# Deeper softmax lookahead in the attention and another order around the first mLSTM chunk, in a two-layer hybrid encoder step

## The reference

```python
def _attend(q, k, v, bias, sinks):
    s = jnp.einsum('...qkgd,...skd->...kgqs', q.astype(jnp.float32), k.astype(jnp.float32))
    s = s * (B_HEAD_DIM ** -0.5) + bias
    sink = jnp.broadcast_to(sinks.astype(jnp.float32)[:, :, None, None], s.shape[:-1] + (1,))
    p = jax.nn.softmax(jnp.concatenate([s, sink], axis=-1), axis=-1)[..., :-1]
    return jnp.einsum('...kgqs,...skd->...qkgd', p, v.astype(jnp.float32))
...
    num = jnp.einsum('nhts,nshd->nthd', s, v) + w_prev.transpose(0, 2, 1)[..., None] * jnp.einsum('nthd,nhde->nthe', q, c_m)
    den = s.sum(axis=-1) + w_prev * jnp.einsum('nthd,nhd->nht', q, n_m)
    norm = jnp.maximum(jnp.abs(den), jnp.exp(-m_t))
    h = num / norm.transpose(0, 2, 1)[..., None]
...
    c_new = decay[..., None, None] * c_m + jnp.einsum('nhs,nshd,nshe->nhde', ws, k, v)
```

## Time and profile before

| | us |
|---|---|
| median of 3 runs (lowest, highest) | 2728.79 (2726.03, 2731.42) |
| the profiled execution | 2728.37 |
| its span, from first to last instruction | 2726.6 |
| PE busy in it | 2655.8 |

### The profile page before, as it was taken

The page is one execution under the profiler, slowest core; times in us unless marked ns, Lnnn a source line. Parts: engine busy times, 40 slices in busy tenths (PEclk is TensorE's granted clock), DMA queues, the critical chain, the costliest instruction groups (busy, mean ns, idle before and its releaser), DMA issues.

```text
span 2726.6 us, 40949 instructions
## 1 busy us (share of the span) xinstructions
PE 2655.8 (97%) x17188; PEld 2591.4 (95%) x17188; DVE 1452.7 (53%) x2384; ACT 605.0 (22%) x1276; POOL 942.2 (35%) x439
## 2 busy tenths in 40 slices
PE   8997999999999999999999989999999999999997
PEld 7896799999999999999999967899999999999997
DVE  7976654444444444657764048654444444444566
ACT  4544331000000000133122147431000000000043
POOL 3321223333333333333433310124333333333430
PEclk9998999999999999999999999999999999999999
DMA  4101211111111111113132232411111111111111
GB/s 144 50 24 56 72 39 47 47 47 47 47 47 47 47 47 47 47 47 127 41 92 93 93 103 84 141 32 55 47 41 45 47 47 47 47 47 47 54 40 64
DMA packets 65487, 162.48 MB, mean 60 GB/s; under 512 B 7696, under 2 KB 36368, under 8 KB 64408
## 3 DMA queue, kind: packets, MB, share of 16 engines
q1 hardware_dynamic: 34224, 114.12, 13.3%
q10 hardware_dynamic: 31080, 45.75, 5.0%
HBM read 139.43 MB, written 20.42 MB: 59 GB/s over the span
## 4 chain that ended last, share of the span: by engine, by line
PE 89%; DVE 5%; ACT 2%; issue 2%; DMA 0%; ACTq 0%; POOL 0%; DVEq 0%; POOLq 0%
PE ps L449 29%; PE ps L451 28%; PE ps L450 28%; PE ps L965 1%; DVE uc L1285 1%; PE ps L690 1%; PE ps L672 1%; DVE ss L1372 1%; DMA ob<-vod 0%; PE ps L895 0%; DVE lr L1308 0%; PE ps L930 0%; PE ps L551 0%; ACT dw L2075 0%; PE ps L656 0%
## 5 line engine op out<-in xcount | busy, mean ns | idle before, releaser
L449 PE MATMUL ps<-xh,wh 128*128 128x352 f32 x3432 | 1119.3, 326 | 21.5 <-DVE xl L1001 12.6
L450 PE MATMUL ps<-xl,wh 128*128 128x352 f32 x3432 | 1112.4, 324 | 0.0
L451 PE MATMUL ps<-xh,wl 128*128 128x352 f32 x3432 | 1112.3, 324 | 0.0
L528 POOL TENSOR_TENSOR wh<-raw,seeds 128x1024 fp32r<-128x1024 f32 x199 | 407.2, 2046 | 1460.2 <-PE ps L451 1424.6
L449 PEld LDWEIGHTS ps<-xh,wh 128*128 128x128 f32 x3432 | 649.9, 189 | 29.7 <-issue 24.3
L450 PEld LDWEIGHTS ps<-xl,wh 128*128 128x128 f32 x3432 | 650.0, 189 | 1.7
L451 PEld LDWEIGHTS ps<-xh,wl 128*128 128x128 f32 x3432 | 649.7, 189 | 0.0
L530 POOL TENSOR_TENSOR wl<-raw,wh 128x1024 fp32r<-128x1024 f32 x208 | 525.3, 2526 | 133.6 <-ACT wh L1693 110.0
L1116 DVE TENSOR_TENSOR tmpa<-ps,rstd 128x352 f32<-128x352 f32 x132 | 69.1, 524 | 719.7 <-PE ps L451 710.8
L449 PE MATMUL ps<-hh,wh 128*128 128x352 f32 x1056 | 340.4, 322 | 0.0
L451 PE MATMUL ps<-hh,wl 128*128 128x352 f32 x1056 | 340.0, 322 | 0.0
(11 more groups left out here) (265 smaller groups left out, 2340.6 us busy)
## 6 DMA issues: line engine op xcount, KB each, us to landing
raw<-wstream SPq DMA_DIRECT2D x208, 512.0 KB, 3.6
vod<-stage ACTq DMA_DIRECT2D x72, 128.0 KB, 1.9
vb<-vod ACTq DMA_DIRECT2D x9, 512.0 KB, 4.1
ob<-vod ACTq DMA_DIRECT2D x9, 512.0 KB, 4.4
x<-xT ACTq DMA_DIRECT2D x2, 2112.0 KB, 8.3
xsave<-x ACTq DMA_DIRECT2D x1, 4224.0 KB, 13.1
x<-xsave ACTq DMA_DIRECT2D x1, 4224.0 KB, 12.6
yT<-ybuf SPq DMA_DIRECT2D x6, 704.0 KB, 3.3
```

The lines of the kernel that those rows point to most:

```text
L449: pe.matmul(out, whi, mhi, start=first, stop=False)
L450: pe.matmul(out, whi, mlo, start=False, stop=False)
L451: return pe.matmul(out, wlo, mhi, start=False, stop=last)
L528: pool.tensor_tensor(hi, raw[:, r, :], zero, ALU.add).then_inc(hi_made, 1)
```

## The change

1. **Attention.** `scores` run two blocks ahead of the transposes rather than one; ss gets four buffers (`ss[h % 4]`) and `biased(h)` waits for the transposes of h - 4. The order on DVE and ACT follows; fill 7 moves from behind block 1 to the A place of block 2, fill 14 and 13 one place forward. `maxima` takes two instructions in place of three, with the sinks negated once beforehand (`nsink`). POOL's splits in the attention stay POOL's.
2. **First mLSTM chunk.** `load_v(0)` and `load_decays(0)` are issued before the O half of the V/O phase; `load_o(0)` goes behind `powers(0)`. POOL's `mask(1)` comes right behind `mask(0)`, ahead of the splits of two weight blocks. The four `c_o` DMAs go from ACT's queue to SP's.
3. **End of the mLSTM.** The last chunk's transposes stand behind unit 2 of the output projection, not behind unit 1.

```diff
-        FILL_A = {0: 4, 1: 6, 4: 9, 5: 11, 6: 12, 7: 13}
-        FILL_B = {0: 5, 1: 7, 3: 8, 4: 10, 7: 14, 8: 15}
+        FILL_A = {0: 4, 1: 6, 2: 7, 4: 9, 5: 11, 6: 12, 7: 14}
+        FILL_B = {0: 5, 3: 8, 4: 10, 6: 13, 8: 15}
...
+                    if NRAW * i + j == B1_OUT + NW:
+                        sp.wait_ge(cup_read, 1 + 8)
+                        for half in range(2):
+                            for f in range(2):
+                                sp.dma_start(half_tile(O["c_o"][1], half, f), state_half(cs, half, f)).then_inc(c_sent, 16)
...
                 if b == B1_OUT + 2:
                     mask(0)
+                    mask(1)
...
-                    if last_chunk is not None and u == 2:
+                    if last_chunk is not None and u == 3:
                         pe.wait_ge(cl_ready, 1 + 2 * (CH - 1))
                         transpose_h(last_chunk)
...
                     transpose_p(2 * n)
-                    if n + 1 < NQ:
-                        scores(n + 1)
+                    if n + 2 < NQ:
+                        scores(n + 2)
                     transpose_p(2 * n + 1)
...
-                step(dve.scalar_tensor_tensor(r[0], r[0], 0.125, sink, ALU.mult, ALU.max))
-                step(dve.tensor_scalar(r[1], r[0], -1.0, None, ALU.mult))
-                dve.tensor_tensor(r[2], sink, r[0], ALU.subtract).then_inc(nm_ready, 1)
+                step(dve.scalar_tensor_tensor(r[1], r[0], -0.125, nsink[0:w, 4 * kvh:4 * kvh + 4], ALU.mult, ALU.min))
+                dve.tensor_tensor(r[2], sink, r[1], ALU.add).then_inc(nm_ready, 1)
...
             for n in range(NQ):
-                a, b = 2 * n + 2, 2 * n + 3
                 if n + 1 < NQ:
-                    biased(a)
-                    maxima(a)
-                    biased(b)
+                    shares(2 * n + 2)
+                if n + 2 < NQ:
+                    biased(2 * n + 4)
+                    maxima(2 * n + 4)
+                if n + 1 < NQ:
+                    shares(2 * n + 3)
                 filled(FILL_A.get(n))
-                if n + 1 < NQ:
-                    maxima(b)
-                    shares(a)
+                if n + 2 < NQ:
+                    biased(2 * n + 5)
+                    maxima(2 * n + 5)
...
             for n in range(NQ):
                 copy_p(2 * n)
                 copy_p(2 * n + 1)
+                if n == 0:
+                    exps(2)
+                    exps(3)
...
-                if n + 1 < NQ:
-                    exps(2 * n + 2)
+                if n + 2 < NQ:
+                    exps(2 * n + 4)
...
             for half, func in ((0, ACT.Copy), (1, ACT.Sigmoid)):
+                if half == 1:
+
+                    for j in range(2):
+                        act.wait_ge(stage_out[j], 16 + 16 * CH * 2)
+                    load_v(0)
+                    act.wait_ge(arow_sent, 16)
+                    load_decays(0)
...
             act.wait_ge(acc_free, FREE0["vo1"] + 72)
             keys_queries(0)
             powers(0)
+            for j in range(2):
+                act.wait_ge(stage_out[j], 16 + 16 * CH * 4)
+            load_o(0)
             chunk(0, None, 1)
```

More of the change, by code:

```diff
@@ L166, in build @@
         lr4 = at("lr4", o_x + 4 * TOK + 2 * CA, [P, CA])
-        ss = at("ss", m, [P, 2, 4, 2 * P])
+        ss = [at(f"ss{i}", off, [P, 4, 2 * P]) for i, off in enumerate((m, m + 1024, m + 4400, m + 8100))]
         pts = at("pts", m + 2048, [P, 2, 8, P])
-        sm = at("sm", m + 4352, [P, 2, 6, 4])
+        sm = at("sm", m + 4096, [P, 4, 6, 4])
         ga = at("ga", o_x, [P, 4, TOK])
@@ L512, in _ @@
                     mask(0)
+                    mask(1)
                 if b == B1_OUT + NW:
-                    for n in range(1, CH):
+                    for n in range(2, CH):
                         mask(n)
@@ L703, in attention @@
                 fill(2)
+                scores(1)
                 fill(3)
@@ L1359, in maxima @@
                 dve.wait_ge(s_read, h + 1)
-                r = [sm[0:w, kvh, j, :] for j in range(6)]
-                step(dve.scalar_tensor_tensor(r[0], r[0], 0.125, sink, ALU.mult, ALU.max))
-                step(dve.tensor_scalar(r[1], r[0], -1.0, None, ALU.mult))
-                dve.tensor_tensor(r[2], sink, r[0], ALU.subtract).then_inc(nm_ready, 1)
+                r = [sm[0:w, h % 4, j, :] for j in range(6)]
+                step(dve.scalar_tensor_tensor(r[1], r[0], -0.125, nsink[0:w, 4 * kvh:4 * kvh + 4], ALU.mult, ALU.min))
+                dve.tensor_tensor(r[2], sink, r[1], ALU.add).then_inc(nm_ready, 1)
             def shares(h):
-                kvh, w = h % 2, q_cols(h // 2)[1]
-                r = [sm[0:w, kvh, j, :] for j in range(6)]
+                w = q_cols(h // 2)[1]
+                r = [sm[0:w, h % 4, j, :] for j in range(6)]
                 dve.wait_ge(exp_done, h + 1)
@@ L1420, in _ @@
             maxima(0)
-            fill_out(1)
             biased(1)
             maxima(1)
+            fill_out(1)
+            shares(0)
             fill_out(2)
-            shares(0)
+            shares(1)
+            biased(2)
+            maxima(2)
+            biased(3)
+            maxima(3)
             fill_out(3)
-            shares(1)
             for n in range(NQ):
-                a, b = 2 * n + 2, 2 * n + 3
                 if n + 1 < NQ:
-                    biased(a)
-                    maxima(a)
-                    biased(b)
+                    shares(2 * n + 2)
[4 more added lines that the diff above has]
+                    shares(2 * n + 3)
                 filled(FILL_A.get(n))
-                if n + 1 < NQ:
-                    maxima(b)
-                    shares(a)
+                if n + 2 < NQ:
+                    biased(2 * n + 5)
+                    maxima(2 * n + 5)
                 if n < NT:
@@ L1441, in _ @@
                     first_out_low()
-                filled(FILL_B.get(n))
                 if n in LOW_O and n < NQ - 1:
                     out_low(n)
-                if n + 1 < NQ:
-                    shares(b)
+                filled(FILL_B.get(n))
             out_low(NQ - 1)
@@ L1904, in exps @@
             def exps(h):
-                kvh, w = h % 2, q_cols(h // 2)[1]
+                w = q_cols(h // 2)[1]
                 act.wait_ge(nm_ready, h + 1)
-                act.activation(sm[0:w, kvh, 3, :], sm[0:w, kvh, 2, :], ACT.Exp)
+                act.activation(sm[0:w, h % 4, 3, :], sm[0:w, h % 4, 2, :], ACT.Exp)
                 for g in range(4):
-                    ins = act.activation(ss[0:w, kvh, g, :], ss[0:w, kvh, g, :], ACT.Exp, bias=sm[0:w, kvh, 1, g:g + 1],
-                                         scale=0.125, accum_out=sm[0:w, kvh, 4, g:g + 1])
+                    sg = ss[h % 4][0:w, g, :]
+                    ins = act.activation(sg, sg, ACT.Exp, bias=sm[0:w, h % 4, 1, g:g + 1], scale=0.125,
+                                         accum_out=sm[0:w, h % 4, 4, g:g + 1])
                 ins.then_inc(exp_done, 1)
@@ L1961, in _ @@
                     out_high(n)
-                    exps(2 * n + 3)
+                if n + 2 < NQ:
+                    exps(2 * n + 5)
             out_high(NQ - 1)
@@ L2116, in chunk @@
                     keys_queries(nxt)
[L2117 to L2121, removed]
                     act.activation(seeds[:, 7:8], seeds[:, 0:1], ACT.Exp)
                     powers(nxt)
[L2125 to L2131, removed]
             act.wait_ge(acc_free, FREE0["vo1"] + 72)
```

29 lines of the change are left out of this document (16 added, 13 removed).

## The result

The changed kernel takes **2707.24 us** (median of 4 runs, 2705.75 to 2708.21), the kernel before 2730.11 (4 runs, 2726.03 to 2732.68): a ratio of 0.9917, 95% interval 0.9900 to 0.9934. The spans of the two profiled executions are 2726.6 and 2706.4 us, 20.2 apart. So it is faster, inside the range on record (2704 to 2721), but 5.8 us under the forecast of 2713.0 and outside the likeliest case's own range (2709 to 2717).

A forecast was written before the change was run, and what follows sets the result against it. PE was taken as the bound, busy 97% of the span, so only its waits and lower clock could be won. Gains of 6.2 + 8.0 + 1.6 = 15.8 us gave 2713.0 us, range 2704 to 2721.

The forecast's parts named there:

- likeliest case: The forecast of 2713.0 us for the whole kernel, with chance 0.50 and its own range 2709 to 2717.
- three new waits of the attention: PE waits 5.5 us at fill(5), 3.9 before the second transposes of n=2 and 3.2 at n=3.
- 6.8 us from `front(0)` to `within(0)`: First mLSTM chunk: with the loads moved, within(0) follows as in the steady chunk, at 1587.14 instead of 1593.87 us.
- (b): Attention gains nothing, reads of each fill behind two shares costing what the depth brings: 2719.2 us, chance 0.17.
- (c): Moved loads don't help, another wait holds the first chunks as long; gain there about 3, time 2718 us, chance 0.09.
- (d): Slower: the fills' reads lag in the whole attention; at 2.4 us each the time is 2739 us, chance 0.04.
- rival (a): The port doesn't hold DVE up in chunk 0; the first chunk then gives 13.5 us, time 2707.5, chance 0.20.
- Part 1: Layer 0's attention: the new queue order has fewer waits and ends 6.2 us earlier; bounds 0 and -15.
- layout of the old order: Attention's engine queues laid out before the change: 147.3 us, of which 112.1 work, 26.3 waits, 8.9 lower clock; ends at 316.6.
- Part 2: First mLSTM chunk: moved loads start within(0) earlier, but POOL's splits delay DVE's four hb; within(1) 8.0 us earlier.
- bound of -13.5: First mLSTM chunk: nothing holds within(1) up and PE, standing less, also keeps its clock; otherwise -12.0.
- Part 3: Last transposes of the mLSTM: one more projection unit ahead of them removes PE's 1.56 us wait, -1.6 us.

The follow-up runs named there:

- x1: Kernel before with only the attention change; loads, mask(1), c_o and last transposes as before: 2721.93 us, ratio 0.9974 to the kernel before.
- x4: Changed kernel with the last chunk's transposes behind unit 1 of the output projection again: 2711.51 us, ratio 0.9942 to the kernel before.
- x11: Changed kernel with mask(1) behind the splits and the c_o DMAs on ACT again: 2711.42 us, ratio 0.9932 to the kernel before.
- x6: Changed kernel with ACT's copy_p(4) ahead of exps(7) and copy_p(6) ahead of exps(9): 2707.61 us, ratio 0.9922 to the kernel before.
- x2: Changed kernel with mask(1) back behind the splits of two weight blocks: 2706.61 us, ratio 0.9919 to the kernel before.
- x3: Changed kernel with the four c_o DMAs issued by ACT again: 2710.72 us, ratio 0.9936 to the kernel before.
- x7: Changed kernel with POOL's first three output-projection splits held until shares(3), (4) and (5) are out: 2702.25 us, ratio 0.9905 to the kernel before.
- x9: Changed kernel with those three splits held, DVE's read of fill(4) first and mask(1) behind the splits: 2704.73 us, ratio 0.9905 to the kernel before.
- x10: Changed kernel with splits held, fill(4) read first, mask(1) behind the splits, copies of head groups 4 and 6 first: 2701.08 us, ratio 0.9893 to before.

## Why the prediction was right, and where its numbers were off

- **Direction and mechanism.** Faster, by all three parts, each where it was laid. The three new waits of the attention, the 6.8 us from `front(0)` to `within(0)` and the missing wait at the end came as written. Rivals (b), (c) and (d) are out. The time itself is outside the likeliest case's own range and inside the range on record because that reaches below rival (a).
- **Part 1, -6.2, measured -7.3.** The term was near, its working less so. The layout of the old order had 26.3 us of waits and 8.9 of lower clock and met the row's end within 0.4 us; the trace has 22.5 us of idle time. The 121.2 us of busy time are 108.2 of the layout's work (its 112.1 less the `fill` ahead of `scores(0)`) and 13.0 of lower clock. So both shares were wrong and offset each other. No run shows the 8.9 us, nor that they stay: the new order has 18.4 idle (laid out: 20.1) and, reckoned in the same way, 9.8 of lower clock, 3.2 less. A total that agrees did not test the parts. The 7.3 are no fixed size either: of six executions with this attention (the change, x1 to x4, x11) five took 136.25 to 136.53 us and one 133.62. x6 shows the price: the layout expected 2.5 to 3.5 us there, and there was nothing.
- **Part 2, -8.0, measured -10.6 at `within(1)` and -11.9 a chunk later.** This is the mis-sized term, though less than it looks: against x1, which has before's order here without its lower clock, the 10.6 are 9.0. The step that failed is "But mask(1) now stands ahead of two splits on POOL. ACT issues its load at about 1588.9". In the change's time that would be 1581.6, with the mask at 1586.1; the load was issued at 1580.11 and the mask ran at 1583.66. The splits thus began 2.5 us earlier. They caught L1626, which the prediction had freed (1.65 us lost; mask(1) itself held L1625 for another 0.6, and the second state half came at 1587.58 instead of 1585.4), and only two POOL instructions were left for the four `hb`: 4.46 us instead of 9.2. `within(1)` came at 1595.74 instead of 1598.3. The path failed with it: the prediction has `within(1)` wait for the last `hb`, but `hb` ended 0.26 us before `sw(1)` could start, and x2 shows them off the path. What the exclusion did cost here is the 1.5 us at the second state half. The last 1.3 us are chunk 1 itself, now free of lower clock, which the prediction had only in its bound of -13.5.
- **"ACT's 3.42 us of `c_o` issues are off this path"** is refuted by x3 and x11. It held only while `hb` was taken to end at 1604.8 (1597.5 in the change's time), and `hb` ended at 1594.64.
- **Part 3, -1.6, measured -1.9**, and 2.8 where the reload of x is slow (x4).
- **Rival (a), 2707.5.** Its time is what was measured; its mechanism is not, and that the numbers meet is luck: it has 13.5 us in part 2, where 11.9 were measured, and less than measured in parts 1 and 3. It said that POOL doesn't hold DVE up in chunk 0. x2 shows that it does. The Trainium skill's rule (SBUF — State Buffer, "Who interferes with whom") stands: the trace agrees, with 1.81 against 0.16 us and 4.46 against 1.67.
- **What is left.** The medians differ by 22.9 us, the profiled executions by 20.2. The profiled execution of before (2728.37) lies 1.7 us under its median and that of the change (2708.21) 1.0 over: these are the 2.7 us. Before's medians in the later runs were 2727.94 to 2729.80; no run here tells more.

## What to carry to other kernels

Check a layout of queues against the measured idle and busy time of a stretch, not against its end alone: two errors can meet the end. Work of GpSimd that nobody needs yet belongs where VectorE reads PSUM or waits (DVE's eight updates of cs, which read PSUM and one SBUF tile, took 3.23 us beside the splits in the change and 3.23 with POOL idle in x2), and putting it later can be worse than leaving it: here it had a free place of 8.6 us, and mask(1) ahead of it pushed it out. When one wait goes, list again what was called off the path, since it was off it only behind that wait; and a slow instruction costs only what waits for it, as the 4.46 us of `hb` show.

## What the runs showed of the hardware

- **The lower clock isn't the same from execution to execution of the same waits.** Behind 3.65 us of standing at 228 us PE's transposes took 1.94 us in one execution and 1.06 in another, and the attention's busy time was 118.0 and 115.2 us. In x7 PE kept 2.4 GHz right behind stands of 2.96, 3.67 and 2.93; in x9 `scores(4)` took 3.48 us behind a stand of 2.38. Six executions of the same attention lie 2.9 us apart, so one profile can't judge an edit that moves waits to better than that.
- **The reload of x** (4224 KB) took 12.6 to 12.8 us in some executions and 13.7 or 13.8 in others (x1, x4, x7, x10); `ob` behind it, which landed in 12.4 or 12.5 us instead of 11.4, came 1 us later with it, and so did PE's last transposes where they wait for it (x1, x4).
- **A small DVE instruction pays as much as a large one.** 128x4 elements took 2.31, 2.24 and 2.26 us beside a POOL instruction of 2.34 to 2.40 us, and ended within 0.03 us of its end; alone they take 0.16.
